# One product with ones, after an addition on VectorE, for the convolution's sum of squares in a decoder layer

## What is computed

```python
def rmsnorm(x, w):
    xf = x.astype(jnp.float32)
    y = xf * lax.rsqrt(jnp.mean(xf * xf, axis=-1, keepdims=True) + EPS)
    return (y * w.astype(jnp.float32)).astype(x.dtype)

y_conv = rmsnorm(short_conv_mixer(b_gate, c_gate, v_conv, conv_w[l]), conv_norm_w[l])
y_hgrn = hgrn2_mixer(q_h, f_h, i_h, g_h, lb_all[l], hgrn_norm_w[l])
x = x + jnp.concatenate([y_conv, y_hgrn], axis=-1) @ w_out[l]
kv = mem_n @ wkv
```

## Time and profile before

| what | before |
|---|---|
| time, median of 3 runs (lowest to highest) | 1653.02 us (1652.17 to 1654.55) |
| the profiled execution: its own time, its span | 1652.41 us, 1650.7 us |
| TensorE busy with products | 1625.9 us, 99% of the span |
| GpSimd busy | 831.8 us, 50% |
| VectorE busy | 1121.2 us, 68% |
| ScalarE busy | 672.5 us, 41% |

### The profile page before, as it was taken

How to read it: one execution, slowest core, us unless ns; L and a number is a source line. 1 busy time by engine, 2 the same in 40 slices (tenths; PEclk the granted TensorE clock), 3 DMA queues, 4 the chain that set the end, 5 groups by cost and what they waited for, 6 DMA issues and landing times.

```text
span 1650.7 us, 26840 instructions
## 1 busy us (share of the span) xinstructions
PE 1625.9 (99%) x9355; PEld 1454.9 (88%) x9355; DVE 1121.2 (68%) x2177; ACT 672.5 (41%) x992; POOL 831.8 (50%) x509
## 2 busy tenths in 40 slices
PE   8999999999999999999999999999999999999998
PEld 6888888788999999999999999998888888888886
DVE  4155442251193999996988888218888888888886
ACT  5352443442334343534444444434333333333333
POOL 4463376413155888996866666766522222222221
PEclk9999999999999999999999999999999999999999
DMA  5222243213635998997999999959999999999991
GB/s 185 96 90 77 84 135 113 90 40 127 224 121 184 322 334 286 317 318 225 333 345 356 355 355 350 326 182 334 397 377 340 344 338 349 344 341 339 349 335 71
DMA packets 153311, 422.15 MB, mean 256 GB/s; under 512 B 15776, under 2 KB 65952, under 8 KB 153120
## 3 DMA queue, kind: packets, MB, share of 16 engines
q1 hardware_dynamic: 90096, 234.52, 41.4%
q0 software_dynamic: 39168, 142.62, 24.4%
q10 hardware_dynamic: 23984, 44.23, 6.9%
HBM read 376.60 MB, written 44.17 MB: 255 GB/s over the span
## 4 chain that ended last, share of the span: by engine, by line
PE 71%; issue 16%; POOL 9%; DMA 2%; ACT 1%; DVE 0%; POOLq 0%; ACTq 0%; DVEq 0%; SPq 0%
PE psum L1445 22%; PE psum L1447 22%; PE psum L1446 22%; POOL w_low L455 8%; PE psum L1736 4%; DMA kept<-down_in 1%; POOL arena L487 1%; PE psum L1721 1%; ACT w_high L578 0%; DMA arena<-gate_dram 0%; DMA arena<-arena 0%; POOL attn_v_low L462 0%; PE psum L1417 0%; PE psum L1764 0%; PE psum L1431 0%
## 5 line engine op out<-in xcount | busy, mean ns | idle before, releaser
L455 POOL TENSOR_TENSOR w_low<-kept,w_high 128x1024 fp32r<-128x1024 f32 x212 | 519.9, 2456 | 371.6 <-ACT w_high L578 370.4
L1445 PE MATMUL psum<-hT_high,w_high 128*128 128x368 f32 (+2 forms) x1408 | 488.8, 347 | 9.7 <-POOL w_low L455 7.9
L1447 PE MATMUL psum<-hT_high,w_low 128*128 128x368 f32 (+2 forms) x1408 | 480.3, 341 | 0.0
L1446 PE MATMUL psum<-hT_low,w_high 128*128 128x368 f32 (+2 forms) x1408 | 480.1, 341 | 0.0
L578 ACT ACTIVATE w_high<-kept 128x1024 fp32r<-128x1024 f32 x212 | 223.9, 1058 | 187.4 <-DMA kept<-down_in 72.3
L1447 PE MATMUL psum<-up_high,wgt_low 128*128 128x512 f32 x768 | 299.1, 390 | 0.0
L1445 PE MATMUL psum<-up_high,wgt_high 128*128 128x512 f32 x768 | 299.1, 389 | 0.0
L1446 PE MATMUL psum<-up_low,wgt_high 128*128 128x512 f32 x768 | 299.1, 389 | 0.0
L1445 PEld LDWEIGHTS psum<-hT_high,w_high 128*128 128x128 f32 x1408 | 264.9, 188 | 25.3 <-POOL w_low L455 12.8
L1446 PEld LDWEIGHTS psum<-hT_low,w_high 128*128 128x128 f32 x1408 | 265.1, 188 | 9.7 <-issue 0.5
L1447 PEld LDWEIGHTS psum<-hT_high,w_low 128*128 128x128 f32 x1408 | 264.7, 188 | 10.2
(11 more groups left out here) (247 smaller groups left out, 1999.9 us busy)
## 6 DMA issues: line engine op xcount, KB each, us to landing
kept<-down_in SPq DMA_DIRECT2D x128, 512.0 KB, 5.6
arena<-up_in SPq DMA_DIRECT2D x128, 512.0 KB, 6.1
kept<-front_w SPq DMA_DIRECT2D x100, 512.0 KB, 3.3
hid_dram<-arena ACTq DMA_DIRECT2D x112, 184.0 KB, 5.7
arena<-hid_dram SPq DMA_DIRECT2D x112, 184.0 KB, 5.3
gate_dram<-arena ACTq DMA_DIRECT2D x40, 512.0 KB, 7.5
under_w<-gate_dram SPq DMA_DIRECT2D x24, 640.0 KB, 8.6
arena<-gate_dram SPq DMA_DIRECT2D x8, 640.0 KB, 8.5
```

The costliest lines, as they stand in the source:

```text
L455: nc.gpsimd.tensor_tensor(w_low[:, s, :], ring[:, s, :], w_hi[:, s, :].bitcast(F32), ALU.subtract).then_inc(low_ready, 1)
L1445: nc.tensor.matmul(out, lhs[0], rhs[0], start=first, stop=False)
L1446: nc.tensor.matmul(out, lhs[0], rhs[1], start=False, stop=False)
L1447: return nc.tensor.matmul(out, lhs[1], rhs[0], start=False, stop=last)
```

## The change

The first three squares are added up in `pC[:, 0]` by VectorE, one addition before tile 3 of the convolution, one behind it, and the third behind the first head's two halves. One product with ones stands in place of four. It is issued behind key block 31, it writes bank 4, and the wait of the values for `conv_root` is gone. ScalarE's copy of key block 31, with the rounded half of block 33 in it, now stands ahead of Ln and Exp.

```diff
-        conv_y, conv_sq, conv_sum, conv_root = (sem(n) for n in ("conv_y", "conv_sq", "conv_sum", "conv_root"))
+        conv_y, conv_sq, conv_total, conv_sum, conv_root = (sem(n) for n in ("conv_y", "conv_sq", "conv_total", "conv_sum", "conv_root"))
...
             keys_out(30, 2)
+            keys_out(31, 3)
             act.wait_ge(conv_sum, 1)
-            step(nc.scalar.activation(junk[:, 0:SEQ], psum[:, 2, :], ACT.Ln, bias=eps))
+            step(nc.scalar.activation(junk[:, 0:SEQ], psum[:, 4, :], ACT.Ln, bias=eps))
             nc.scalar.activation(junk[:, SEQ:2 * SEQ], junk[:, 0:SEQ], ACT.Exp, scale=-0.5).then_inc(conv_root, 1)
-            keys_out(31, 3)
...
+            def add_square(c):
+                dve.wait_ge(conv_sq, c + 1)
+                return nc.vector.tensor_tensor(pC[:, 0, :], pC[:, 0, :], pC[:, c, :], ALU.add)
+
+            step(add_square(1))
             conv(3)
             step.end()
+            step(add_square(2))
             dve.wait_ge(block_used, 28)
             for h in range(HH):
                 y_halves(CC + h, rinv[:, h, :])
+                if h == 0:
+                    add_square(3).then_inc(conv_total, 1)
...
             keys(30, 2)
-            pe.wait_ge(conv_sq, CC)
+            keys(31, 3)
+            pe.wait_ge(conv_total, 1)
+            nc.tensor.matmul(psum[:, 4, :], ones, pC[:, 0, :], start=True, stop=True).then_inc(conv_sum, 1)
             pe.wait_ge(o_root, HH)
-            for c in range(CC):
-                ins = nc.tensor.matmul(psum[:, 2, :], ones, pC[:, c, :], start=(c == 0), stop=(c == CC - 1))
-            ins.then_inc(conv_sum, 1)
-            keys(31, 3)
-            pe.wait_ge(conv_root, 1)
             values(32, 2)
```

## The result

The launch takes 1655.56 us with the change (median of 20 runs, 1653.91 to 1660.32) and 1653.91 before (20 runs, 1651.39 to 1657.44). The ratio is 1.0014, 95% interval 1.0008 to 1.0020: 1.3 to 3.3 us slower, which reaches but does not pass the 0.2% that had been called no change. The ratio is taken over all launches; the two medians alone lie 1.65 us apart.

A forecast was written before the change was run, and what follows sets the result against it. TensorE, busy 99% of the span, was taken as the bound. Terms: -2.58 products, +1.9 block 31's low half, +0.14 late first product, +3.1 block 35's low half, -1.07 stall before block 37: +1.5 us, 1654.5; range 1650.9 to 1657.4.

The forecast's parts named there:

- Three products less: TensorE's products with ones: three fewer at 0.86 us each, 2.58 us less, the upper end of the edit's own gain.
- Block 31 waits for its low half: TensorE ready at 204.05, key block 31 starts at 205.9 behind GpSimd's low half; 1.9 of the 2.58 us become a wait.
- the tie against the third addition: At 203.36 VectorE's third addition asks just as GpSimd begins block 31's low half; GpSimd goes first, addition done at 206.3.
- The rule that stood beside the sum: Shared port as exclusive lock: third addition goes first, block 31's low half some 0.6 us later, sum about +1.3.
- The additions delay the scalings and with them the last value block: VectorE's first scaling ends at 216.65, before 212.94; block 35, the last value block, starts at 221.05, waiting about 3 us.
- a sign of being wrong: The prediction called itself wrong if the last value block starts without a wait, or the projection starts before 235.
- The chain of waits: TensorE waits 1.9 us before key block 31 and 3.1 before the last value block; projection at about 236.5, 1.5 late.
- ScalarE's waits before L687: ScalarE's waits before its roundings of the convolution's output, on VectorE's scalings, should grow by some 3 us.
- Full size to the end of the launch: Behind the change TensorE is nearly always busy, so the shift at the stretch's end carries to the launch's end undiminished.
- VectorE slips through: Rival: VectorE wins ties against GpSimd, first scaling by 213.5; gain 0.54 to 1.6 us, 1651.4 on the median's scale; chance 0.20.
- one more low half: Rival: a VectorE scaling ends one GpSimd low half later, TensorE stops 2.4 to 2.85 us more; +4.35, 1657.4; chance 0.12.

The follow-up runs named there:

- the filled kernel: The changed kernel plus two unread products ahead of key block 31, where TensorE waits for a low half; 1655.91 us, ratio to before 1.0011.
- four products late: The kernel before with its four products behind key block 31, in bank 4, ScalarE in the change's order, no additions on VectorE; 1658.68 us, ratio 1.0029.
- the additions alone: The kernel before, four products kept, plus the change's three VectorE additions into a row nobody reads; 1657.16 us, ratio 1.0016.
- the repeats: The changed kernel profiled two more times, nothing altered, for the clock; stretch from tile 3's last instruction to the projection 36.96 and 36.75 us.

## Why the prediction was right, and where not

The forecast was 1.5 us slower, no change by 0.2%. Measured are 1.3 to 3.3 us. Of its steps:

- **Three products less, 2.58 us.** Right in price: from the product with ones at 211.13 to the values' second product at 212.22, less the 0.23 between two of these, it cost 0.86, and in the filled kernel (209.10 to 210.19) 0.86 again.
- **Block 31 waits for its low half, 1.9 us.** The stop was 2.39 in all three profiles of the change. The step took GpSimd to win the tie against the third addition; the addition won, and the low half took 2.91 us instead of 2.40. Half of that 0.51 us was not the tie: with no additions, in the run with four products late, it took 2.65 and the stop was 2.06. The rule that stood beside the sum, the exclusive lock of the Trainium skill ("SBUF — State Buffer", on who interferes with whom), gave the order of the two and some 0.6 us for it, against the 0.5 measured; here the trace agrees with it.
- **The additions delay the scalings and with them the last value block.** Shown by the additions alone: +1.38 us on the stretch against +1.5 forecast. In the repeats the stop before that block was 2.24 and 2.23 us, where 3.1 had been forecast: TensorE came there later, because of the longer first stop, but the block began at 220.90 and 220.62 against 221.05. The first scaling began at 215.77; it had been forecast to end at 216.65. In the first profile of the change it came another way, by block 38, for the reason above: the last value block began without a wait, which the prediction had named as a sign of being wrong. The chain of waits was right for two of three profiles. ScalarE's waits before L687, which were to grow by some 3 us, are 5.84 us in sum before, 5.51 in the first profile and 6.88 in a repeat.
- **The missing term is the clock.** The prediction counted stops at their own length. In three of three profiles of the change the granted clock fell to half behind one of its two stops: block 31 took 4.44 us instead of 2.95. 1.4 us from the chain and 1.5 from the clock make the 2.9 of the stretch (36.89 less 34.00); in the first profile, whose chain was another, that split is worked out from the other runs. This is what the sum should have had beside its +1.5. That the medians, 1.65 us apart, lie so near to 1.5 is therefore in part luck.
- **Full size to the end of the launch.** From the projection to the end of the span it is 1415.7 us before (1650.7 less 234.97) and 1414.9 after (1653.0 less 238.14). But over the other profiles it goes from 1416.2 to 1421.0, with code that is the same there. A part of that is the clock again: before has one fall in it, near 635 us, the first profile of the change has none behind the projection, and the three longest, 1419.4 (four products late), 1420.2 (the additions alone) and 1421.0 (the filled kernel's repeat), have two falls' worth. So the stretch's 2.9 us agree with the launch's 1.3 to 3.3 within what that part scatters, and a stretch of one profile can't be set against a median to better than 2 or 3 us. The run with the additions alone shows it: +1.38 in the stretch, 3.6 in the medians.
- **Two slips in the working.** The scaling that ScalarE waited 3.69 us for is the third of four, not the last, and it is the third that decides block 37, the fourth block 38. And the 1652.9 of "VectorE slips through" follows from none of its terms: 1652.41 less 1.6 is 1650.8. Neither enters the sum.

Of the rivals, "one more low half" came in part in the first profile: the third and the fourth scaling each ended with one, and TensorE stopped 1.97 us before block 38. But that stop stood in place of the one before the last value block and not on top of it, so its +4.35 did not come. "VectorE slips through" happened in part there too, at the first two scalings, and gave nothing, since the last two were caught.

## What to carry to other kernels

Work that is moved from a busy engine to an idle one is free only if the idle engine's queue holds nothing that others wait for: three additions of 0.69 us cost 1.4 us of the launch's path, since each instruction more in front of the scalings could cost a whole operation of GpSimd. Ask of removed work what wait it had covered; four products stood in a time when the next block's operand was not there. What mended it was taking the casts out of that queue and putting what others wait for at its head, together with fewer products. How much the fewer products give there is not shown: casts on ScalarE and scalings first, with the four products of before, was not run.

## What the runs showed of the hardware that was not expected

**A stop of about 2 us can halve TensorE's clock for some 3 us, and does not always.** Over the profiled executions of this stretch there are fourteen stops on a low half from 1.96 to 3.15 us; behind six of them the clock fell to 1.2 GHz, among them 1.97, 2.06, 2.23, 2.24 and 2.39 us, and behind eight it did not, among them 1.97, 2.24, 2.39 and 3.15. Behind shorter ones (0.34 to 1.68 us) it never fell there. Each fall cost about 1.5 us: 4.44 less 2.95 in block 31, and from the start of the last value block to the projection 17.12 us in a repeat of the change against 15.57 in the first profile of the filled kernel. The Trainium skill, "Advanced Engine Details and Errata", section Clock Domains, says that the array's clock is gated to 1.2 GHz when idle; the rows agree as to the level, and show that the same stop does it in one execution and not in the next.

**The tie at the shared port.** Before, GpSimd began at 209.95 with a VectorE subtraction 0.18 us from its end and lost 0.04 us. After, GpSimd's row begins at 203.63 and VectorE's addition at 203.65, right behind another instruction of VectorE, and GpSimd was the one to wait, 2.91 us against the 2.40 that it takes undisturbed (at 212.89 in a repeat). Two starts 0.02 us apart don't tell who waits; the length of the rows does.
